# First mixing stage: attention heads one portion later, value products directly behind score products

## The chip, the cores and the metric

The kernel runs on one core of one Trainium2 chip. The metric is the device time of one execution in microseconds (us); smaller is better. A core has TensorE (PE in the profile, with its weight loads as PEld), VectorE (DVE), ScalarE (ACT), GpSimd (POOL) and SyncE (SP), which issues the DMAs. Each engine runs its own instructions in order, and they wait for one another by semaphores.

## The reference, cut to what matters

Two transformer blocks on 256 tokens of width 1024, in float32. The change touches only the mixing stage of the first block, `first_block` in the reference:

```python
h = h + 0.5 * swiglu(rmsnorm(h, ffn1_norm[l]), ffn1_w_gu[l], ffn1_w_down[l])
u = rmsnorm(h, mix_norm[l])
qa, ka, va, qb, kb, vb, qi, ki, wi, g = jnp.split(u @ w_in[l], SPLIT_POINTS, axis=-1)
...
out_a = dsa_attention(qa, ka, va, qi, ki, wi, bias_dsa)   # 8 heads of 64, 64 best keys of each query
out_b = moba_attention(qb, kb, vb, bias_moba)             # 8 heads of 64, plain causal at this length
gates = jax.nn.sigmoid((g + b_gate[l]).astype(jnp.float32)).astype(h.dtype)
g_a, g_b = jnp.split(gates, 2, axis=-1)
mixed = g_a * (out_a @ w_branch_dsa[l]) + g_b * (out_b @ w_branch_moba[l])
h = h + mixed @ w_out[l]
h = h + 0.5 * swiglu(rmsnorm(h, ffn2_norm[l]), ffn2_w_gu[l], ffn2_w_down[l])
```

Each of the 16 heads computes softmax(q k^T / 8 + bias) v with a causal mask. The second block has an attention and a recurrence of its own and is not touched.

## The kernel before, in words

All large products are made of three TensorE products of split operands: ScalarE copies a weight unit to `hi` (line 801), VectorE subtracts to get `lo` (line 1253), and TensorE adds hi*xh, lo*xh and hi*xl (lines 1823 to 1825). A unit is 1 MB, three slots go round, and SP loads a unit when `lo` of the unit three before it is done.

The first mixing stage is the product u @ w_in in 11 chunks of columns, each in 4 **portions**, so 44 portions p = 0 to 43. Portion p is chunk p // 4, half p // 2 % 2 of the contraction, and token tile t = p % 2; on TensorE it is 12 matmuls of 512 columns. Everything else of the stage is hung behind a portion number, and each engine has a loop over the same p with its own steps in an order written out by hand:

- `M1_T`: portions behind which q and k rows are transposed (TensorE line 2049, ScalarE line 993 takes them out). I call such a group M. Two of them stand at 21 and 22, two more at 25 and 26.
- `M1_DOTS`, `M1_TOPK`: the index scores and the 8 rounds of max and replace on VectorE, portions 13 to 20, with a threshold at 21.
- `M1_STEP[k]`: the portion of softmax step k; k = 0 to 7 are the heads of `moba_attention`, 8 to 15 those of `dsa_attention`. Before, it is 20 + k.

For step k the work is spread so (before):

- TensorE, portion 20 + k, k even only: `pair_scores` for heads k and k + 1, 8 matmul passes (lines 1978 to 1982) on halves of 64 rows. I call it S. Its waits ask that the logits of the two steps before are done (`m_l`).
- VectorE, portion 20 + k: `logits`, which adds the bias and takes the row maximum (lines 1403 and 1407), increments `m_l`.
- ScalarE, portion 21 + k: the exponential (line 1042).
- VectorE, portion 22 + k: reciprocal and scaling (lines 1597 and 1599), increments `m_n`.
- TensorE, portion 23 + k: three transposes of the probabilities (line 2080), which wait for `m_n`. I call it T. ScalarE copies them to `pt1` (line 1010), in the same portion.
- TensorE, portion 24 + k, k odd only: `pair_values` for heads k - 1 and k, 8 passes (lines 1993 to 1997) on halves of 64 columns. I call it V. It stands in the code behind T.

`M1_MASK[h]` (22 + h) is the portion in which VectorE adds the key mask to the bias of head h (line 1592). `M1_OUT[j]` (28, 32, 36, 40) is where ScalarE and VectorE take four heads' output out of PSUM (lines 1051 and 1607). VectorE's order within a portion is: logits, head scaling of the projections (`head_scale`, line 1525), head sums (line 1517), gate eviction (1573), max rounds, threshold (1585), mask, reciprocal and scaling, output, and last `lo` of half a unit. ScalarE's is: M out, `pt1`, eviction and square of the projections (1032 and 1036), exponential, output, the sigmoid of portion 39, and last `hi` of half a unit. A chunk's eviction runs in its portions with p % 4 = 2 and 3.

So an even portion from 24 on was followed on TensorE by S and T, and an odd one by T and V. TensorE works in three layouts here: the full array (portions, M, T), two halves of rows (S), two halves of columns (V).

Of the kernel before, what the change touches and what calls it, by code (L numbers as in the profile page):

```python
# [47 lines left out]
NH = 8  # L48
# [50 lines left out]
        (4, 0): 21, (4, 1): 22, (5, 0): 25, (5, 1): 26}  # L99
M1_DOTS = 9  # L100
M1_TOPK = 13
M1_STEP = [20 + k for k in range(2 * NH)]
M1_MASK = [22 + h for h in range(NH)]
M1_OUT = [28, 32, 36, 40]

M2_T = {(c, t): 4 * (c + 1) + 1 + t for c in (0, 1, 3, 4, 5, 7, 8, 9) for t in range(NT)}
M2_STEP = [12, 13, 15, 16, 18, 19, 21, 22, 24, 25, 26, 27, 29, 30, 32, 33]
# [10 lines left out]
def at(seq, p):  # L118

    return seq.index(p) if p in seq else -1  # L120
# [12 lines left out]
def key_at(table, p):  # L133

    for key, when in table.items():
        if when == p:
            return key
    return None
# [65 lines left out]
def program(nc, a, out):  # L204
    ctx = ExitStack()
    with ctx:
        def sem(name):
            return ctx.enter_context(nc.semaphore(name))

        def sb(name, shape, dt=F32, where=ctx):  # L210
            return where.enter_context(nc.sbuf_tensor(name, shape, dt))
# [44 lines left out]
        with scope() as s:  # L256
# [6 lines left out]
            v1 = sb("v1", [P, NT, W], F32, s)  # L263
            v1b = sb("v1b", [P, NT, W], F32, s)
# [114 lines left out]
        m_ev = sem("m_ev")  # L379
# [18 lines left out]
        m_ptc = sem("m_ptc")  # L398
        m_pv = sem("m_pv")
        m_oh = sem("m_oh")  # L400
        m_ol = sem("m_ol")
# [373 lines left out]
        def _(act):  # L775
# [197 lines left out]
            for p in range(4 * len(IN1)):  # L973
# [22 lines left out]
                if M1_DOTS <= p < M1_DOTS + NIDX:  # L996
                    h = p - M1_DOTS
                    act.wait_ge(m_dot, h + 1)
                    if h >= 1:
# [3 lines left out]
                                         scale=HD ** -0.5 * NIDX ** -0.5).then_inc(m_relu, 1)  # L1003
                k = at(M1_STEP, p - 3)
                if k >= 0:
# [5 lines left out]
                if u == 1 and kind != "g":  # L1011
# [15 lines left out]
                    else:  # L1027
# [8 lines left out]
                        nc.scalar.activation(sq, hid[:, t, :], ACT.Square).then_inc(m_sq, 1)  # L1036
                k = at(M1_STEP, p - 1)
                if k >= 0:
# [6 lines left out]
                    e.then_inc(m_p, 1)  # L1045
                j = at(M1_OUT, p)
                if j >= 0:
# [174 lines left out]
        def _(dve):  # L1222
# [304 lines left out]
            for p in range(4 * len(IN1)):  # L1527
# [3 lines left out]
                if M1_DOTS <= p < M1_DOTS + NIDX:  # L1531
# [11 lines left out]
                    dve.wait_ge(m_acc, 2 * h + 2)  # L1543
                k = at(M1_STEP, p)
                if k >= 0:
# [37 lines left out]
                if p == M1_TOPK + TOPK // 8:  # L1583

                    step(nc.vector.tensor_scalar(score[:, :], score[:, :], (FILL + TAKEN) / 2, NEG,
                                                 ALU.is_gt, ALU.mult))
                h = at(M1_MASK, p)
                if h >= 0:
# [3 lines left out]
                    nc.vector.tensor_tensor(bias_a[:, h, :], bias_a[:, h, :], score[:, :], ALU.add).then_inc(m_masked, 1)  # L1592
                k = at(M1_STEP, p - 2)
                if k >= 0:
# [6 lines left out]
                    ins.then_inc(m_n, 1)  # L1601
                j = at(M1_OUT, p)
                if j >= 0:
# [196 lines left out]
        def _(pe):  # L1800
            def use(n, off=0):
                pe.wait_ge(lo_done, n + 1 + RING * off)
# [47 lines left out]
            def turned(r, t, b):  # L1850

                pe.wait_ge(n_xl, 4 * r + ROUNDS[r].index((t, b)) + 1)
# [122 lines left out]
            def pair_scores(qt, qb, kt, kb, done):  # L1975

                upper, lower = slice(0, HD), slice(HD, 2 * HD)
                nc.tensor.matmul(S[0][:, 0:SEQ], qt[upper, qb, P:SEQ], kt[upper, kb, :], start=True, stop=True)  # L1978
                nc.tensor.matmul(S[1][:, 0:SEQ], qt[lower, qb, P:SEQ], kt[lower, kb, :], start=True, stop=True)
                nc.tensor.matmul(S[0][:, SEQ:SPAN], qt[upper, qb, 0:P], kt[upper, kb, 0:P],  # L1980
                                 start=True, stop=True).then_inc(done, 1)
                nc.tensor.matmul(S[1][:, SEQ:SPAN], qt[lower, qb, 0:P], kt[lower, kb, 0:P],
                                 start=True, stop=True).then_inc(done, 1)

            def pair_values(v, k):

                h = k % NH
                o = O[h // 4]
                first = h // 2 % 2 * SEQ
                whole, late = slice(first, first + SEQ), slice(first + P, first + SEQ)  # L1990
                left, right = slice(h * HD, h * HD + HD), slice(h * HD + HD, h * HD + 2 * HD)
                one, two = pt1[:, k % 4, :], pt1[:, k % 4 + 1, :]
                nc.tensor.matmul(o[0:HD, whole], v[:, 0, left], one[:, 0:SEQ], start=True, stop=False)  # L1993
                nc.tensor.matmul(o[HD:P, whole], v[:, 0, right], two[:, 0:SEQ], start=True, stop=False)
                nc.tensor.matmul(o[0:HD, late], v[:, 1, left], one[:, SEQ:SPAN],
                                 start=False, stop=True).then_inc(m_pv, 1)
                nc.tensor.matmul(o[HD:P, late], v[:, 1, right], two[:, SEQ:SPAN],
                                 start=False, stop=True).then_inc(m_pv, 1)
# [13 lines left out]
            for p in range(4 * len(IN1)):  # L2012
                c, u, t = p // 4, p // 2 % 2, p % 2
                if c == 0:

                    u, t = p % 2, p // 2
                    turned(1, t, u)
                _, width, kind = IN1[c]
                n = U_M1 + 2 * c + u
                if t == 0:  # L2020
                    use(n)
                if u == 0 and c > 0:

                    if c <= 7:
                        pe.wait_ge(m_ev, 2 * (c - 1) + t + 1)
                    else:
                        pe.wait_ge(m_gadd, 2 * (c - 8) + t + 1)
                ins = portion(n, t, G[t], xh, xl, 4 * u, u == 0, u == 1, width)
                if t == 1:
                    ins.then_inc(used, 1)  # L2030
                elif u == 1:
                    ins.then_inc(m_g0, 1)
                if c == 0 and t == 0:
                    turn_norm(1, 2 + u)
                key = key_at(M1_T, p)
                if key is not None:
                    cc, tt = key
                    order = list(M1_T).index(key)
                    if order >= 1:
                        pe.wait_ge(m_trev, order)  # L2040
                    if cc == 0:
                        pe.wait_ge(m_ev, tt + 1)
                        for j in range(3):
                            ins = nc.tensor.transpose(X[0][:, j * P:(j + 1) * P], idx[:, tt, j * P:(j + 1) * P],
                                                      ident[:, :])
                    else:
                        pe.wait_ge(m_qn, 2 * (1, 2, 4, 5).index(cc) + tt + 1)
                        for j in range(4):
                            ins = nc.tensor.transpose(X[0][:, j * P:(j + 1) * P], hid[:, tt, j * P:(j + 1) * P],
                                                      ident[:, :])  # L2050
                    ins.then_inc(m_tr, 1)
                if M1_DOTS <= p < M1_DOTS + NIDX and (p - M1_DOTS) % 2 == 0:

                    h = p - M1_DOTS
                    pe.wait_ge(m_trev, 2)
                    if h == 0:
                        pe.wait_ge(res_done, 4)
                    else:
                        pe.wait_ge(m_relu, h)
                    pair_scores(idxt, h // 2, idxt, 2, m_dot)  # L2060
                k = at(M1_STEP, p)
                if k >= 0 and k % 2 == 0:

                    if k == 0:
                        pe.wait_ge(m_relu, NIDX)
                        pe.wait_ge(m_trev, 6)
                    else:
                        pe.wait_ge(m_l, k)
                    if k == NH:
                        pe.wait_ge(m_trev, 10)  # L2070
                    qt, kt = (q_m, k_m) if k < NH else (q_a, k_a)
                    pair_scores(qt, k % NH // 2, kt, k % NH // 2, m_s)
                k = at(M1_STEP, p - 3)
                if k >= 0:

                    pe.wait_ge(m_n, k + 1)
                    if k >= 1:
                        pe.wait_ge(m_ptc, k)
                    for j, b in enumerate((2, 0, 1)):
                        ins = nc.tensor.transpose(PT[:, j * P:(j + 1) * P], l1[:, k % 4, b * P:(b + 1) * P],  # L2080
                                                  ident[:, :])
                    ins.then_inc(m_pt, 1)
                k = at(M1_STEP, p - 4)
                if k >= 0 and k % 2 == 1:

                    pe.wait_ge(m_ptc, k + 1)
                    if k == 1:
                        pe.wait_ge(m_ev, 8)
                    if k == NH + 1:
                        pe.wait_ge(m_ev, 14)  # L2090
                    if k >= NH and k % 4 == 1:
                        pe.wait_ge(m_ol, (k - NH) // 4 + 1)
                    pair_values(v1 if k < NH else v1b, k - 1)


            for q in range(4):
# [40 lines left out]
            for p in range(4 * len(IN2)):  # L2137
# [30 lines left out]
                k = at(M2_STEP, p)  # L2168
                if k >= 0 and k % 2 == 0:
                    h = k // 2  # L2170
# [107 lines left out]
```

## Time and profile before

| | us |
|---|---|
| median of 3 runs | 1003.91 (1003.77 to 1003.92) |
| the profiled execution | 1003.34 |
| its span | 1001.5 |
| PE busy | 992.6 (99%) |
| DVE busy | 688.5 (69%) |
| ACT busy | 548.8 (55%) |

The granted TensorE clock is 1.00 of full speed in the whole execution. The page's 40 slices show PE at 9 tenths in all but the first and the last. The first mixing stage lies between about 205 and 342 us of the span. The timelines give the start and the duration of each instruction; as matmuls overlap, the cost of one is read from the distance of starts and not from its duration.

### The profile page before, as it was taken

What the parts mean: (1) busy time and instruction counts of PE and PEld (TensorE: products, weight loads), DVE (VectorE), ACT (ScalarE), POOL (GpSimd) and SP (SyncE); (2) the same over time, 40 slices, a digit from 0 to 9 for tenths busy, and PEclk for the clock granted to TensorE, in tenths of its full rate; (3) what the DMA queues carried; (4) which work ended last, traced back from release to release, by engine and by line L of the source; (5) the groups of instructions that cost most, each with busy time, mean ns of one, the idle gap of its engine ahead of it and who ended that gap; (6) DMA issues with size and microseconds to landing.
All of it is one profiled execution on the core that took longest, in us unless ns stands there. A gap on an engine that the chain in (4) does not pass through costs nothing.

```text
span 1001.5 us, 12563 instructions
## 1 busy us (share of the span) xinstructions
PE 992.6 (99%) x4626; PEld 814.0 (81%) x4626; DVE 688.5 (69%) x1008; ACT 548.8 (55%) x749; POOL 120.4 (12%) x109
## 2 busy tenths in 40 slices
PE   8999999999999999999999999999999999999998
PEld 7788888888777888888888887888888888888887
DVE  6656666668977567656565667787689767656663
ACT  7444443566766536444444576768875545444541
POOL 0000000022200000000000041258913000000000
PEclk9999999999999999999999999999999999999999
DMA  7987776585434636656666466467556546787761
GB/s 261 296 248 254 236 245 211 194 288 179 143 127 128 208 126 216 226 184 225 198 210 223 134 252 216 129 188 207 150 171 208 195 154 219 224 221 227 224 196 43
DMA packets 158953, 199.87 MB, mean 200 GB/s; under 512 B 49585, under 2 KB 105018, under 8 KB 158778
## 3 DMA queue, kind: packets, MB, share of 16 engines
q1 hardware_dynamic: 158890, 199.24, 62.8%
q8 instruction: 29, 0.48, 0.2%
q14 instruction: 18, 0.15, 0.0%
q10 hardware_dynamic: 16, 0.00, 0.0%
HBM read 182.45 MB, written 5.77 MB: 188 GB/s over the span
## 4 chain that ended last, share of the span: by engine, by line
PE 93%; DVE 3%; DMA 1%; ACT 1%; POOL 1%; issue 0%; SPq 0%; ACTq 0%
PE bank L1823 22%; PE bank L1825 22%; PE bank L1824 22%; PE bank L1928 7%; PE bank L1926 7%; PE bank L1927 7%; PE bank L1836 1%; DMA raw<-in_w_in 1%; PE bank L1978 1%; DVE lo L1253 1%; PE bank L2080 1%; POOL rstd_q L718 1%; PE bank L1993 0%; DMA resid<-in_x 0%; DVE ss_q L1517 0%
## 5 line engine op out<-in xcount | busy, mean ns | idle before, releaser
L1823 PE MATMUL bank<-hi,xh 128*128 128x512 f32 (+1 forms) x944 | 375.4, 398 | 1.4 <-DVE xl L1275 0.8
L1825 PE MATMUL bank<-hi,xl 128*128 128x512 f32 (+1 forms) x944 | 367.1, 389 | 0.0
L1824 PE MATMUL bank<-lo,xh 128*128 128x512 f32 (+1 forms) x944 | 366.6, 388 | 0.0
L1236 DVE TENSOR_TENSOR lo<-raw,hi 128x2048 fp32r<-128x2048 f32 x112 | 256.2, 2289 | 147.9 <-ACT hi L792 147.9
L792 ACT ACTIVATE hi<-raw 128x2048 fp32r<-128x2048 f32 (+1 forms) x116 | 220.5, 1903 | 133.1 <-PE bank L1928 97.0
L1823 PEld LDWEIGHTS bank<-hi,xh 128*128 128x128 f32 x944 | 177.4, 188 | 40.3 <-issue 2.2
L1825 PEld LDWEIGHTS bank<-hi,xl 128*128 128x128 f32 x944 | 177.2, 188 | 37.5
L1824 PEld LDWEIGHTS bank<-lo,xh 128*128 128x128 f32 x944 | 177.6, 188 | 34.5
L1253 DVE TENSOR_TENSOR lo<-raw,hi 128x1024 fp32r<-128x1024 f32 (+1 forms) x108 | 132.4, 1233 | 32.4 <-ACT hi L801 31.6
L1926 PE MATMUL bank<-hi,hh 128*128 128x512 f32 x304 | 118.9, 391 | 0.0
L1928 PE MATMUL bank<-hi,hl 128*128 128x512 f32 x304 | 118.3, 389 | 0.0
L1927 PE MATMUL bank<-lo,hh 128*128 128x512 f32 x304 | 118.3, 389 | 0.0
L801 ACT ACTIVATE hi<-raw 128x1024 fp32r<-128x1024 f32 x100 | 104.0, 1050 | 16.0 <-PE bank L1825 11.7
L866 ACT ACTIVATE hh<-hid_t 128x512 fp32r<-128x512 f32 x34 | 20.7, 629 | 92.6 <-DVE hid_t L1304 92.6
L1928 PEld LDWEIGHTS bank<-hi,hl 128*128 128x128 f32 x304 | 57.1, 188 | 11.9
L1927 PEld LDWEIGHTS bank<-lo,hh 128*128 128x128 f32 x304 | 57.1, 188 | 11.7
L1926 PEld LDWEIGHTS bank<-hi,hh 128*128 128x128 f32 x304 | 57.1, 188 | 11.5
L711 POOL TENSOR_TENSOR small<-small 128x1 f32<-128x1 f32 x10 | 8.4, 848 | 371.7 <-DVE small L1260 353.4
L854 ACT ACTIVATE act_out<-bank,small 128x256 f32<-128x256 f32 x44 | 20.9, 475 | 55.9 <-PE bank L1825 55.2
L718 POOL TENSOR_TENSOR rstd_q<-ss_q,small 128x8 f32<-128x8 f32 x16 | 37.4, 2336 | 90.9 <-DVE ss_q L1519 90.9
L1312 DVE TENSOR_TENSOR hl<-hid_t,hh 128x512 fp32r<-128x512 f32 x34 | 22.9, 691 | 20.8 <-ACT hh L866 20.8
L1287 DVE SCALAR_TENSOR_TENSOR hid<-bank,small,act_out 128x256 f32<-128x256 f32 x44 | 21.1, 480 | 15.1 <-ACT act_out L854 15.1
(262 smaller groups left out, 958.9 us busy)
## 6 DMA issues: line engine op xcount, KB each, us to landing
raw<-in_w_in SPq DMA_DIRECT2D x48, 1024.0 KB
raw<-in_ffn_w_gu SPq DMA_DIRECT2D x84, 512.0 KB
raw<-in_ffn_w_down SPq DMA_DIRECT2D x22, 1024.0 KB
raw<-in_w_up SPq DMA_DIRECT2D x16, 1024.0 KB
raw<-in_w_down SPq DMA_DIRECT2D x16, 1024.0 KB
raw<-in_w_out SPq DMA_DIRECT2D x8, 1024.0 KB
distance_table<-ftab SPq DMA_DIRECT2D x8, 576.0 KB
raw<-in_w_proj_attn SPq DMA_DIRECT2D x4, 1024.0 KB
```

What stands on the lines that cost most here:

```text
L718: nc.gpsimd.tensor_tensor(rstd_q[:, s], ss_q[:, s], minus_half[:, 0:8], ALU.pow).then_inc(rstd_sem, 1)
L792: nc.scalar.activation(hi[s][:, :, 0:width], raw[s][:, :, 0:width], ACT.Copy).then_inc(hi_done, 1)
L801: ins = nc.scalar.activation(hi[s][:, cut, :], raw[s][:, cut, :], ACT.Copy)
L1236: nc.vector.tensor_tensor(lo[s][:, :, 0:width], raw[s][:, :, 0:width], hi[s][:, :, 0:width].bitcast(F32), ALU.subtract).then_inc(lo_done, 1)
L1253: ins = nc.vector.tensor_tensor(lo[s][:, cut, 0:width], raw[s][:, cut, 0:width], hi[s][:, cut, 0:width].bitcast(F32), ALU.subtract)
L1312: nc.vector.tensor_tensor(hl[:, kt, :], hid_t[:, kt, :], hh[:, kt, :].bitcast(F32), ALU.subtract).then_inc(f.hl, 1)
L1823: nc.tensor.matmul(o, sh, wh, start=first and j == 0, stop=False)
L1824: nc.tensor.matmul(o, sh, wl, start=False, stop=False)
L1825: ins = nc.tensor.matmul(o, sl, wh, start=False, stop=last and j == 3)
L1926: nc.tensor.matmul(DB[t][h][:, :], sh, wh, start=begin, stop=False)
L1927: nc.tensor.matmul(DB[t][h][:, :], sh, wl, start=False, stop=False)
L1928: ins = nc.tensor.matmul(DB[t][h][:, :], sl, wh, start=False, stop=end)
```

## The change

Three lists of portion numbers move by one or two, and in TensorE's loop the V block is put in front of the T block and behind portion `M1_STEP[k] + 5` in place of `+ 4`.

```diff
-M1_STEP = [20 + k for k in range(2 * NH)]
-M1_MASK = [22 + h for h in range(NH)]
-M1_OUT = [28, 32, 36, 40]
+M1_STEP = [21 + k for k in range(2 * NH)]
+M1_MASK = [23 + h for h in range(NH)]
+M1_OUT = [30, 34, 38, 42]
...
                     pair_scores(qt, k % NH // 2, kt, k % NH // 2, m_s)
-                k = at(M1_STEP, p - 3)
-                if k >= 0:
-
-                    pe.wait_ge(m_n, k + 1)
-                    if k >= 1:
-                        pe.wait_ge(m_ptc, k)
-                    for j, b in enumerate((2, 0, 1)):
-                        ins = nc.tensor.transpose(PT[:, j * P:(j + 1) * P], l1[:, k % 4, b * P:(b + 1) * P],
-                                                  ident[:, :])
-                    ins.then_inc(m_pt, 1)
-                k = at(M1_STEP, p - 4)
+                k = at(M1_STEP, p - 5)
                 if k >= 0 and k % 2 == 1:
                     pe.wait_ge(m_ptc, k + 1)
...
                     pair_values(v1 if k < NH else v1b, k - 1)
+                k = at(M1_STEP, p - 3)
+                if k >= 0:
+
+                    pe.wait_ge(m_n, k + 1)
+                    if k >= 1:
+                        pe.wait_ge(m_ptc, k)
+                    for j, b in enumerate((2, 0, 1)):
+                        ins = nc.tensor.transpose(PT[:, j * P:(j + 1) * P], l1[:, k % 4, b * P:(b + 1) * P],
+                                                  ident[:, :])
+                    ins.then_inc(m_pt, 1)
```

After it, S stands behind the odd portions 21 to 35, T behind 24 to 39, V behind the odd portions 27 to 41. Behind portions 27, 29, 31, 33 and 35 TensorE has S, V, T in this order, and behind the even ones between them T alone. The instructions and their number are the same.

## Rows read from the trace of the kernel before

**Rows 1.** The page: busy us of each engine, share of the span, instructions.

```profile
PE 992.6 (99%) x4626; PEld 814.0 (81%) x4626; DVE 688.5 (69%) x1008; ACT 548.8 (55%) x749; POOL 120.4 (12%) x109
```

**Rows 2.** Timeline of PE behind portions 28 and 29: start, duration, instruction [idle before].

```profile
283.89 0.50 PE L1823 MATMUL bank<-hi,xh 128*128 128x512 f32 x1
...
286.86 0.48 PE L1978 MATMUL bank<-k_a,q_a 64*128 64x256 f32 x1
...
287.51 0.27 PE L1982 MATMUL bank<-k_a,q_a 64*128 64x128 f32 x1
287.71 0.55 PE L2080 MATMUL bank<-ident,l 128*128 128x128 f32 x3
288.01 0.48 PE L1823 MATMUL bank<-hi,xh 128*128 128x512 f32 x1
...
291.28 0.43 PE L1993 MATMUL bank<-pt,v 128*64 128x256 f32 x1
...
292.08 0.50 PE L1823 MATMUL bank<-hi,xh 128*128 128x512 f32 x1
```

**Rows 3.** Timeline of PE, starts of portions 36 and 37.

```profile
316.58 0.50 PE L1823 MATMUL bank<-hi,xh 128*128 128x512 f32 x1
...
319.68 0.48 PE L1823 MATMUL bank<-hi,xh 128*128 128x512 f32 x1
```

**Rows 4.** Timeline of PE where the heads begin, portions 21 to 24.

```profile
257.32 0.60 PE L2049 MATMUL bank<-ident,hid 128*128 128x128 f32 x4
257.67 0.48 PE L1823 MATMUL bank<-hi,xh 128*128 128x512 f32 x1
...
260.53 0.60 PE L2049 MATMUL bank<-ident,hid 128*128 128x128 f32 x4
261.80 0.48 PE L1978 MATMUL bank<-k_m,q_m 64*128 64x256 f32 x1 [0.67 <-DVE small L1407]
...
265.99 0.55 PE L2080 MATMUL bank<-ident,l 128*128 128x128 f32 x3 [0.32 <-DVE l L1599]
...
270.41 0.55 PE L2080 MATMUL bank<-ident,l 128*128 128x128 f32 x3 [0.28 <-DVE l L1599]
```

**Rows 5.** Timeline of DVE in the same stretch.

```profile
256.98 0.42 DVE L1403 CUSTOM_DVE_ANT_0 l<-bank,bias_m 128x256 f32<-128x256 f32 x1
...
259.76 1.23 DVE L1253 TENSOR_TENSOR lo<-raw,hi 128x1024 fp32r<-128x1024 f32 x1
260.90 0.41 DVE L1403 CUSTOM_DVE_ANT_0 l<-bank,bias_m 128x256 f32<-128x256 f32 x1
...
266.98 0.42 DVE L1403 CUSTOM_DVE_ANT_0 l<-bank,bias_m 128x256 f32<-128x256 f32 x1
...
267.73 0.68 DVE L1525 TENSOR_TENSOR hid<-hid,rstd_q 128x512 f32<-128x512 f32 x1
268.34 0.69 DVE L1517 TENSOR_REDUCE ss_q<-act_out 128x8 f32<-128x512 f32 x1
...
269.14 0.55 DVE L1592 TENSOR_TENSOR bias_a<-bias_a,score 128x384 f32<-128x384 f32 x1
269.61 0.16 DVE L1597 RECIPROCAL small<-small 128x2 f32<-128x2 f32 x1
```

**Rows 6.** Timeline of ACT in the same stretch.

```profile
257.95 0.69 ACT L993 ACTIVATE q_a<-bank,cols 128x512 f32<-128x512 f32 x1 [3.73 <-PE bank L2049]
258.66 1.28 ACT L1042 ACT_TABLE_LOAD   x1
259.95 0.51 ACT L1042 ACTIVATE l<-l,small 128x256 f32<-128x256 f32 x1
...
260.85 1.04 ACT L801 ACTIVATE hi<-raw 128x1024 fp32r<-128x1024 f32 x1
...
262.36 0.67 ACT L1032 ACTIVATE hid<-bank,small 128x512 f32<-128x512 f32 x1
263.07 0.63 ACT L1036 ACTIVATE act_out<-hid 128x512 f32<-128x512 f32 x1
```

**Rows 7.** Timeline of DVE: its first wait once the heads run.

```profile
279.64 0.42 DVE L1403 CUSTOM_DVE_ANT_0 l<-bank,bias_m 128x256 f32<-128x256 f32 x1 [1.30 <-PE bank L1982]
```

More of the change, by code:

```diff
@@ L2072, in _ @@
                     pair_scores(qt, k % NH // 2, kt, k % NH // 2, m_s)
+                k = at(M1_STEP, p - 5)
+                if k >= 0 and k % 2 == 1:
+                    pe.wait_ge(m_ptc, k + 1)
+                    if k == 1:
+                        pe.wait_ge(m_ev, 8)
+                    if k == NH + 1:
+                        pe.wait_ge(m_ev, 14)
+                    if k >= NH and k % 4 == 1:
+                        pe.wait_ge(m_ol, (k - NH) // 4 + 1)
+                    pair_values(v1 if k < NH else v1b, k - 1)
                 k = at(M1_STEP, p - 3)
@@ L2082, in _ @@
                     ins.then_inc(m_pt, 1)
-                k = at(M1_STEP, p - 4)
[L2084 to L2093, printed above, removed]
             for q in range(4):
```

## The prediction

> **What bounds the kernel now.** I read the page first: TensorE is busy 99% of the span and no other engine passes 69% [rows 1]. So a microsecond of TensorE time, work or stall, is one of the kernel, unless something else then ends last. The change adds and removes no instruction, which leaves two things to look for: what TensorE pays for passing from one array layout to another, and where it stands idle. The timeline of PE answers both.
>
> In the steady part [rows 2] the last score pass starts at 287.51 and the transposes 0.20 later, at 287.71, though that pass has only 128 columns, against the 512 that a portion's matmul moves in 0.23: S pays an exit. Going in costs too: from the first matmul of portion 28 (283.89) to the first score pass (286.86) are 2.97, where 12 matmuls of about 0.23 would take 2.73, and 0.13 to 0.16 of the rest is the slower first matmul behind V. T and the entry into V are still dearer: the values start at 291.28, 3.27 behind the portion's first matmul at 288.01, and the next portion starts 0.80 behind them (292.08).
>
> Where the heads begin, TensorE waits three times [rows 4]: S of step 2 (261.80) waits 0.67 for the logits, T of step 0 (265.99) and T of step 1 (270.41) wait 0.32 and 0.28 for the scaled probabilities. Counted from the start of their portions with the distances above, the two T are late by 0.47 and 0.35, so the three waits cost 1.5 in all. They end at VectorE, whose timeline has no gap in this stretch [rows 5]; its first wait comes at 279.64 [rows 7]. So in the steady part TensorE sets the pace, and in the fill, 255 to 275 us, VectorE does. The two halves of the change must be costed there separately.
>
> **Part 1: V next to S, steady part.** Before, a pair of portions costs 292.08 - 283.89 = 8.19 [rows 2]: S, T, then T, V. After, an odd portion has S, V, T and an even one T alone. T alone is a row: 319.68 - 316.58 = 3.10 [rows 3]. The odd one is put together: portion up to S 2.95 (2.97 less a little, since a portion now follows T and not V), S from first to last pass 0.65, then x for the step from row halves to column halves, V 0.60 from first to last pass and 0.20 out (0.80 together), T to the next portion 0.30 (288.01 - 287.71). That is 4.70 + x, and the pair 7.80 + x. The gain is 0.39 - x.
>
> No row shows x. Its low end is 0, V starting on top of the last score pass; its high end is 0.40, two exits of 0.20 in a row. The nearest row is the exit from S into T, also a change of layout from the same passes, 0.20 [rows 2]. I take 0.21. The gain is then about 0.17 for a pair, and S and V meet behind five portions: 0.85. Behind 37 and 39, V then T takes what T then V took, since each has one entry and one exit of V: no gain, no loss. With the ends of x, Part 1 is worth between 0 and 1.9.
>
> On this the Trainium skill, "TensorEngine Tiling (Array Packing)", section Key Properties, says that a change of tiling mode drains TensorE. The 0.20 exits agree. By that rule S to V, from 64 by 128 to 128 by 64, is again a drain, so one change of four is saved and not two: it speaks for x near 0.20 and against its low end.
>
> **Part 2: everything one portion later, the fill.** One could hope that VectorE, which is behind because of the max rounds (portions 13 to 20), catches up when the heads come one portion later, and that the 1.5 of waits goes. I follow the instructions.
>
> TensorE: portion 21 starts without S of step 0 in front of it. M of portion 21, then S, and portion 22 starts at 257.6, where it also started before (257.67) [rows 4], as S has only changed places with M. M of portion 22 is at 260.5, portion 23 starts 0.35 behind it (257.67 - 257.32) at 260.84. S of step 2 comes at 263.8, and VectorE has the logits of step 1 by then: it starts portion 20's work at 256.98, now without the 0.75 of logits, so `lo` of portion 20 starts at 259.0 (259.76 less 0.75) and ends at 260.15; logits of step 0 (0.75), the threshold, `lo` (1.14) and logits of step 1 (0.75) follow, done by about 263.2 [rows 5]. The wait of 0.67 is gone. Portion 24 starts at 264.6, and T of step 0 could be issued at 267.5.
>
> ScalarE: the exponential of step 0 moves from portion 21 to portion 22. In portion 21 there was nothing between M's copy and it; portion 22 also holds an eviction and a square. And the first exponential brings the table load of 1.28 with it [rows 6]. So, in portion 22: M's copy 0.63 behind M (257.95 - 257.32), 261.1; eviction 261.7; square 0.71 later (263.07 - 262.36), 262.4; table load 262.9; exponential 1.29 later, 264.2; `hi` 0.90 later (260.85 - 259.95), 265.1; it ends at 266.2. ScalarE was idle before that, from its `hi` of portion 21, done at about 258.4, to 261.1, but its queue is in order and the load stands behind M's copy.
>
> VectorE: it has done head sums of portion 22 at 264.0, and its next instruction is `lo` of portion 22, which needs that `hi`. It starts at 266.2, not at 264.0: 2.2 idle, and the lead is spent. `lo` takes 1.14 (260.90 - 259.76): 267.3. Then, for portion 23, by the distances of rows 5: logits of step 2 0.75 (268.1), head scaling 0.61 (268.7), head sums 0.80 (269.5), mask 0.47 (270.0), reciprocal and scaling to the transposes 0.80 (270.41 in rows 4 less 269.61): T of step 0 starts at 270.8. TensorE could have at 267.5, so it waits 3.3.
>
> Before, the portion of VectorE that T of step 0 waited for had no head scaling in it. So this T comes about when T of step 1 came before (270.41 [rows 4]).
>
> After that I find no stall: S of step 4 at 274.5 needs logits of step 3 (272.5); T of step 1 at 275.3 could start from 274.4; T of step 2 at 278.9 has its input at about 277.3; from then on VectorE is 1 to 2 ahead at every T. In the odd portions ScalarE now stays longer behind T (V is in front of it), so `hi` and `lo` come some 1 later, but they are due four portions ahead. At the end, sigmoid and T meet in ScalarE's portion 39: `lo` for the first unit behind the stage is done near 337.5, 5 before its use. The fill costs 3.3 - 1.5 = 1.8 more.
>
> **Sum.** +1.8 - 0.85 = +0.95; a count of portion starts up to portion 43, with 4.91 and 3.10 in turn, gives +0.85. I take +0.9. Against the profiled execution (1003.34, span 1001.5 and 1.84 around it) this is 1004.2. The median of the runs is 0.57 above the profiled execution, and I forecast the median: 1003.9 + 0.9 = 1004.8.
>
> **The rivals.**
>
> *VectorE catches up.* If the table load is issued while ScalarE is idle before 261.1, or something else lets `hi` of portion 22 come by 264, T of step 0 is ready at 268.6, and the fill wait is 1.1 in place of 3.3. Then the fill gains 0.4, and with Part 1 the time is 1003.9 - 1.25 = 1002.7. If no wait at all is left, 1003.9 - 1.5 - 0.85 = 1001.6. For it: the heads do get 3 us more. Against: both the load and the copy stand in one in-order queue. Chance 0.17 for 1002.7 and 0.07 for 1001.6.
>
> *S next to V buys nothing or costs.* x = 0.40 makes the time 1003.9 + 1.8 = 1005.7. Chance 0.10.
>
> *The wait costs more than itself.* This is the one that ends measurably slower. The longest wait shown on TensorE in the fill is 0.67 [rows 4], with the clock at full level; one of 3.3 is new, and nothing here shows that the granted clock of 2.4 GHz survives it. If the portion behind it ran at 1.2 GHz, 2.9 of work would take 2.9 more: 1007.7. It decides as soon as the wait is long enough for the clock to fall. Chance 0.06. The Trainium skill, "TensorE: Matmul & The Clock Gate", section on HAM oscillation, says that idle gaps between bursts throttle the engine again; no run here shows it. A second chain of the same kind (head sums of portion 23 late as well, so T of step 1 late too) gives 1 to 2 more, 1006.3: chance 0.08.
>
> The forecast itself has 0.52.
>
> **How the numbers follow.** About 0.2%, 2.0 us here, is what a measurement of this kernel can tell from no change. Faster than 1001.9: the last form of the first rival and a little of its neighbour, 0.09. Slower than 1005.9: the clock, the second chain and the edge of x = 0.40, 0.15. The rest, 0.76, is within. The range leaves out the no-wait case below and the clock case above: 1002.1 to 1006.4.
>
> **What would show it.** Right: in PE's timeline one wait of about 3 us at the transposes behind portion 24, released by VectorE's scaling, and no wait at S of step 2; in ACT's, the table load behind the square near 262.9; in DVE's, an idle of about 2 before `lo` of portion 22, released by `hi`; portion pairs from 27 on 8.0 apart, and 0.2 from the last score pass to the first value pass. Wrong: no wait above 1.5 in the fill, a table load before 261, pairs of 8.2 or 7.8, a granted clock below 1.00 near 270, or new waits at portions 28 to 43.

## The result and the profile after

| | us |
|---|---|
| before, median of 15 runs | 1003.60 (1002.98 to 1004.20) |
| after, median of 15 runs | 1005.96 (1004.36 to 1008.00) |
| ratio | 1.0024, 95% interval 1.0017 to 1.0031 |
| after, the profiled execution | 1007.63 (span 1005.8, mean granted clock 0.996) |

The kernel became slower by 2.4 us. The median hides a spread: these 15 runs of before lie within 1.2 us, those of after within 3.6. Every run also lists its mean granted TensorE clock. Five of the 15 executions after have 1.000 and take 1004.36 to 1004.84, median 1004.48. The other ten have 0.996 to 0.998 and take 1005.05 to 1008.00. So there are two costs: 0.9 us that each execution pays, and up to 3.5 more that only some pay.

The page of the profiled execution, which is one of the slower kind: the busy line that answers to [rows 1], and, in 40 slices of 25 us, the busy tenths of PE and the granted clock.

```profile
PE 995.2 (99%) x4626; PEld 816.8 (81%) x4626; DVE 689.3 (69%) x1008; ACT 548.6 (55%) x749; POOL 120.1 (12%) x109
...
PE   8999999999899999999999999999999999999998
...
PEclk9999999999899999999999999999999999999999
```

Before, the clock row was all 9. After, it has an 8 in the eleventh slice, 251 to 277 us, and there PE's busy share falls as well. The list of TensorE's waits (us in total, times, longest) shows what is there. The two waits of before at L2080 and the one at L1978 [rows 4] are gone, and one of 3.2 has come (L2091 is the transposes' new line):

```profile
PE bank L2091 <- DVE l L1599: 3.2, 1, 3.2
PE bank L1965 <- POOL small L706: 1.8, 1, 1.8
PE bank L1836 <- DMA resid<-in_x: 1.0, 1, 1.0
```

This execution reaches the stage later than the profiled one before, for nothing that the change touches: the first transposes of the stage (L2044) start at 211.39, before at 210.62. So 0.77 has to be taken off its times before they are laid beside those of before or of the forecast.

The timeline of PE at the start of the heads, against [rows 4]: portion 22 begins at 258.37, S of step 2 at 264.51 has no wait, T of step 0 has the long one, and behind it the matmuls start 0.43 apart in place of 0.23.

```profile
256.99 0.60 PE L2049 MATMUL bank<-ident,hid 128*128 128x128 f32 x4
257.51 0.48 PE L1978 MATMUL bank<-k_m,q_m 64*128 64x256 f32 x1
...
258.37 0.50 PE L1823 MATMUL bank<-hi,xh 128*128 128x512 f32 x1
...
261.23 0.60 PE L2049 MATMUL bank<-ident,hid 128*128 128x128 f32 x4
...
264.51 0.48 PE L1978 MATMUL bank<-k_m,q_m 64*128 64x256 f32 x1
...
271.62 0.90 PE L2091 MATMUL bank<-ident,l 128*128 128x128 f32 x3 [3.23 <-DVE l L1599]
272.18 0.78 PE L1823 MATMUL bank<-hi,xh 128*128 128x512 f32 x1
...
274.03 0.63 PE L1824 MATMUL bank<-lo,xh 128*128 128x512 f32 x1
274.46 0.63 PE L1825 MATMUL bank<-hi,xl 128*128 128x512 f32 x1
...
278.05 0.48 PE L1978 MATMUL bank<-k_m,q_m 64*128 64x256 f32 x1
```

ScalarE's timeline, against [rows 6]: the table load now stands behind the square of portion 22, and `hi` of that portion starts only at 266.00.

```profile
261.86 0.69 ACT L993 ACTIVATE q_a<-bank,cols 128x512 f32<-128x512 f32 x1 [2.60 <-PE bank L2049]
262.45 0.68 ACT L1032 ACTIVATE hid<-bank,small 128x512 f32<-128x512 f32 x1
263.16 0.63 ACT L1036 ACTIVATE act_out<-hid 128x512 f32<-128x512 f32 x1
263.81 1.28 ACT L1042 ACT_TABLE_LOAD   x1
...
266.00 1.04 ACT L801 ACTIVATE hi<-raw 128x1024 fp32r<-128x1024 f32 x1
```

VectorE's timeline, against [rows 5]: it waits 2.23 for that `hi`, and then does head scaling, head sums and mask before the reciprocal at 270.83.

```profile
264.67 0.17 DVE L1519 TENSOR_SCALAR ss_q<-ss_q 128x8 f32<-128x8 f32 x1
267.07 1.23 DVE L1253 TENSOR_TENSOR lo<-raw,hi 128x1024 fp32r<-128x1024 f32 x1 [2.23 <-ACT hi L801]
...
268.96 0.69 DVE L1525 TENSOR_TENSOR hid<-hid,rstd_q 128x512 f32<-128x512 f32 x1
...
270.83 0.16 DVE L1597 RECIPROCAL small<-small 128x2 f32<-128x2 f32 x1
```

The steady part, against [rows 2] and [rows 3]: two portions take 298.69 - 290.69 = 8.00 in place of 8.19, the first value pass starts 0.20 behind the last score pass, and T 0.20 behind the last value pass.

```profile
290.69 0.47 PE L1823 MATMUL bank<-hi,xh 128*128 128x512 f32 x1
...
294.28 0.27 PE L1982 MATMUL bank<-k_a,q_a 64*128 64x128 f32 x1
294.48 0.43 PE L1993 MATMUL bank<-pt,v 128*64 128x256 f32 x1
...
295.08 0.27 PE L1997 MATMUL bank<-pt,v 128*64 128x128 f32 x1
295.28 0.55 PE L2091 MATMUL bank<-ident,l 128*128 128x128 f32 x3
...
298.69 0.47 PE L1823 MATMUL bank<-hi,xh 128*128 128x512 f32 x1
```

Last the clock. The busy times of two stretches of 4 us in the changed kernel; the clock is the number 0.60 and 0.55 ahead of the DMA share. Before, all stretches read 1.00.

```profile
270.00:274.00 4.00, 2.38 (x7) 2.02 (x8) 3.90 (x14) 1.54 (x7) 1.87 (x1) 0.60 0.64 241
274.00:278.00 4.00, 4.00 (x13) 2.97 (x11) 2.28 (x6) 0.87 (x1) 0.00 (x0) 0.55 0.16 19
```

A mean of 0.60 over 4 us is 3.2 us at half the clock, a mean of 0.55 is 3.6. So TensorE went to its lower level of 1.2 GHz at about 270.8, towards the end of the wait, after it had been idle since 268.4. It stayed there for the rest of the wait and the whole portion behind it, 6.8 us in all, and was back at 2.4 GHz by S of step 4.

### The profile page after: what moved, and what is told of

The parts are those of the page before. It is cut to its first block, busy times and chain, and to the rows that moved or that the text cites. A ratio compares the mean times of both kernels' runs of the same rounds, so it can differ in the third digit from the quotient of the medians.

```text
span 1005.8 us, 12563 instructions
## 1 busy us (share of the span) xinstructions
PE 995.2 (99%) x4626; PEld 816.8 (81%) x4626; DVE 689.3 (69%) x1008; ACT 548.6 (55%) x749; POOL 120.1 (12%) x109
## 4 chain that ended last, share of the span: by engine, by line
PE 96%; DVE 1%; ACT 1%; POOL 0%; DMA 0%; issue 0%; SPq 0%; ACTq 0%
PE bank L1823 23%; PE bank L1825 23%; PE bank L1824 23%; PE bank L1928 7%; PE bank L1927 7%; PE bank L1926 7%; PE bank L1836 1%; PE bank L1978 1%; PE bank L2091 1%; PE bank L1993 0%; DMA resid<-in_x 0%; PE bank L2049 0%; PE bank L1980 0%; DVE lo L1253 0%; PE bank L2212 0%; PE bank L2213 0%
```

## The experiments

The first four were measured together with the kernel before (its median: 1003.51 of 31 runs, from 1002.76 to 1005.04), the last three in a second series (1003.64 of 25, from 1002.99 to 1004.56). The kernel before spreads over 2.3 us in the first of these at clocks of 0.999 and 1.000, so a wide spread alone is no sign of a fallen clock; the clock listed with each run is. Each ratio is against the kernel before of the same series.

**The shift alone.** The order of T and V as before, the heads one portion later.

```diff
-M1_STEP = [20 + k for k in range(2 * NH)]
-M1_MASK = [22 + h for h in range(NH)]
-M1_OUT = [28, 32, 36, 40]
+M1_STEP = [21 + k for k in range(2 * NH)]
+M1_MASK = [23 + h for h in range(NH)]
+M1_OUT = [29, 33, 37, 41]
```

> Heads one portion later, but the value products behind the transposes as before (portion M1_STEP + 4, outputs at 29, 33, 37, 41). Theory (fill costs 1.8 more, adjacency gains 0.85): T of step 0 waits about 3.2 us, S of step 2 does not wait, portion pairs stay 8.2 apart; 1005.4 us where the clock stays at full level, 2 to 3 more where it falls, median about 1007. Rival (the shift itself is harmless, the new order of S, V and T costs): 1003.6 us and no clock below 1.00.

Measured: median 1006.48 (1005.16 to 1006.86, 9 runs), ratio 1.0025 [1.0015, 1.0035]. Four runs with clock 1.000 take 1005.16 to 1006.00, five with 0.998 take 1006.48 to 1006.86. The wait is in place, in an execution whose clock stayed at 1.00; there T of step 0 at 271.71 is followed by S of step 4 at 275.39, 3.68 later, where the changed kernel's slowed execution needed 278.05 - 271.62 = 6.43 for the same work.

```profile
271.71 0.55 PE L2080 MATMUL bank<-ident,l 128*128 128x128 f32 x3 [3.23 <-DVE l L1599]
...
275.39 0.48 PE L1978 MATMUL bank<-k_m,q_m 64*128 64x256 f32 x1
```

The whole loss is in the shift, and the clock falls without S and V being neighbours, so the rival, that the new order costs, is out. What was expected of the slower executions did not come: their median lies 1.2 above that of the four with clock 1.000, not 2 to 3, and so the median is 1006.48 and not about 1007. In the changed kernel the same distance is 2.4. Why a fallen clock costs less here is not shown, and the samples are small.

**The new order alone.**

```diff
-M1_STEP = [21 + k for k in range(2 * NH)]
-M1_MASK = [23 + h for h in range(NH)]
-M1_OUT = [30, 34, 38, 42]
+M1_STEP = [20 + k for k in range(2 * NH)]
+M1_MASK = [22 + h for h in range(NH)]
+M1_OUT = [29, 33, 37, 41]
```

(against the changed kernel)

> Heads where they were before (M1_STEP = 20 + k, masks 22 + h), only the value products moved to M1_STEP + 5 in front of the transposes (outputs at 29, 33, 37, 41). Theory: the three short waits of before stay (0.67, 0.32, 0.28 by the profile), five pairs cost 8.0 in place of 8.17 to 8.2, the clock stays at 1.00: 1003.6 - 0.85 = 1002.8 us. Rival (adjacency is what costs or what lets the clock fall): 1003.6 to 1006 us with clocks below 1.00.

Measured: 1002.87 (1002.21 to 1003.45), ratio 0.9993 [0.9984, 1.0002], clocks 0.999 and 1.000. The medians are 0.64 apart, near the 0.85 expected, but the interval holds 1, so by the times alone the gain is not shown. The trace does show its parts: the three waits of before and nothing else, and the portions behind two successive groups of S, V and T start 8.00 apart, at 287.47 and 295.47.

```profile
261.66 0.48 PE L1978 MATMUL bank<-k_m,q_m 64*128 64x256 f32 x1 [0.68 <-DVE small L1407]
265.85 0.55 PE L2091 MATMUL bank<-ident,l 128*128 128x128 f32 x3 [0.31 <-DVE l L1599]
270.27 0.55 PE L2091 MATMUL bank<-ident,l 128*128 128x128 f32 x3 [0.24 <-DVE l L1599]
...
287.47 0.48 PE L1823 MATMUL bank<-hi,xh 128*128 128x512 f32 x1
...
295.47 0.47 PE L1823 MATMUL bank<-hi,xh 128*128 128x512 f32 x1
```

**The wait filled with work.** This and the next three are edits of the changed kernel. Twelve matmuls whose results nothing reads, ahead of the wait of T of step 0.

```diff
                 if k >= 0:

+                    if k == 0:
+                        for d in range(12):
+                            nc.tensor.matmul(O[1][:, :], xh[:, d % 4, 0:P], hi[(U_M1 + 12) % RING][:, d % 4, :],
+                                             start=True, stop=True)
                     pe.wait_ge(m_n, k + 1)
```

> The changed kernel, with 12 more full matmuls (128 rows, 128 by 512, results into a bank that nothing reads) issued by TensorE in front of the wait of T of step 0, so that it computes 2.7 of the 3.3 us in which it would be idle. Theory (the clock falls because TensorE is idle for 3.2 us): granted clock 1.000 in every execution, about 1004.5 us, spread like that of the kernel before (about 1 us). Rival (the clock falls for something else in the new order, or the spread has nothing to do with it): clocks of 0.996 to 0.998 in most executions again, median 1006.

Measured: 1004.29 (1003.85 to 1005.50), ratio 1.0009 [1.0000, 1.0018], clock 1.000 in all 11 runs. The runs lie within 1.7 us, about 1 was expected, and those of before in the same series within 2.3. T of step 0 comes 271.43 - 256.80 = 14.63 behind M of portion 21, exactly as in the changed kernel (271.62 - 256.99), so nothing was saved but the idling:

```profile
268.04 2.88 PE L2089 MATMUL bank<-hi,xh 128*128 128x512 f32 x12
271.43 0.55 PE L2095 MATMUL bank<-ident,l 128*128 128x128 f32 x3 [0.51 <-DVE l L1599]
```

More work on TensorE made the kernel 1.6 us faster (0.8 over the kernel before, in place of 2.4). The lower clock of the changed kernel comes from TensorE standing idle for 3.2 us. What is left is near the forecast of +0.9, but its interval reaches from 0 to 1.8 us.

**The table load moved to where ScalarE is idle.**

```diff
                 mixing_split(split_hi_part, U_M1, p)
+                if p == 21:
+                    nc.scalar.activation(small[:, 23:24], ident[:, 0:1], ACT.Exp)
```

> The changed kernel, with one exponential of a single column more on ScalarE at the end of portion 21, where it is idle, so that the table load of 1.28 us does not stand in portion 22 in front of the first half unit of hi. Theory (hi of portion 22 is late by the table load and by the exponential): VectorE's idle before lo of portion 22 falls from 2.2 to 0.9, T of step 0 waits 1.9 to 2.0 in place of 3.2; 1003.2 us, and the clock stays at 1.00 in all or nearly all executions. Rival (VectorE's own work sets T of step 0): the wait stays above 3 us, 1004.5 to 1006.

Measured: 1002.88 (1002.36 to 1004.37), ratio 0.9993 [0.9984, 1.0002], clocks 0.999 and 1.000. The median is 0.3 under the 1003.2 expected. The load stands at 258.60, VectorE's idle ahead of `lo` of portion 22 is 0.81 (2.23 in the changed kernel), and T of step 0 waits 1.81, a little less than the 1.9 to 2.0 expected:

```profile
258.60 1.28 ACT L1060 ACT_TABLE_LOAD   x1
...
261.19 0.69 ACT L993 ACTIVATE q_a<-bank,cols 128x512 f32<-128x512 f32 x1 [1.09 <-PE bank L2051]
...
263.91 1.04 ACT L801 ACTIVATE hi<-raw 128x1024 fp32r<-128x1024 f32 x1
```

```profile
264.98 1.23 DVE L1255 TENSOR_TENSOR lo<-raw,hi 128x1024 fp32r<-128x1024 f32 x1 [0.81 <-ACT hi L801]
```

`hi` starts 263.91 - 261.19 = 2.72 behind the copy of M of portion 22, in the changed kernel 266.00 - 261.86 = 4.14, so it comes 1.42 earlier. Both idle times fell by 1.42 too: what ScalarE's queue is rid of, VectorE no longer idles and TensorE no longer waits. One instruction on one column is worth 3 us in the median. Of this 1.4 is the wait; the rest is what the clock had cost, the 1.6 that filling the wait gave back as well.

**The scaling right behind the logits.** VectorE's loop, the block for `at(M1_STEP, p - 2)` moved up.

```diff
                     logits(S[k % 2], l1[:, k % 4, :], bias, k, m_l)
+                k = at(M1_STEP, p - 2)
+                if k >= 0:
+                    dve.wait_ge(m_p, k + 1)
+                    step(nc.vector.reciprocal(inv[:, 2 * k:2 * k + 2], sums[:, 2 * k:2 * k + 2]))
+                    ...
+                    ins.then_inc(m_n, 1)
                 if p >= 1 and (p - 1) // 4 in (1, 2, 4, 5) and (p - 1) // 2 % 2 == 1:
                     head_scale(2 * (1, 2, 4, 5).index((p - 1) // 4) + (p - 1) % 2, (p - 1) % 2, m_qn, m_rstd)
```

> The changed kernel, with VectorE's reciprocal and scaling moved from behind head scaling, head sums and mask to right behind the logits of the portion. Theory (T of step 0 waits for a queue in order: those three stand in front of what it needs, 0.61 + 0.80 + 0.47 = 1.9): the wait falls from 3.2 to 1.4, the time to 1002.6 us, and the clock stays at 1.00 as in the kernel with the early table load, whose wait was 1.8. Rival (the scaling itself waits for the exponential, or the displaced work makes a later wait): wait above 2.5, or new waits behind portions 25 to 30; 1003.5 or more.

Measured: 1002.99 (1001.97 to 1003.83), ratio 0.9992 [0.9983, 1.0001], clocks 0.999 and 1.000. The wait is 1.37 as expected, and no other one came; the median is 0.4 over what was expected, within the spread of the runs.

```profile
269.47 0.55 PE L2091 MATMUL bank<-ident,l 128*128 128x128 f32 x3 [1.37 <-DVE l L1564]
```

**Both together**, the two diffs above in one kernel.

> The changed kernel with both: the early table load and the scaling right behind the logits. Theory: the two take 1.4 and 1.9 from the wait of 3.2, so that none is left; no wait of TensorE at all in portions 21 to 43; 1001.1 us, 2.4 below the kernel before (of which 1.5 are its three waits and 0.85 the five pairs). Rival (another input is late next, the max rounds or a head scaling): 1002 us or more, with a named wait in the trace.

Measured: 1001.22 (1000.95 to 1002.28, 9 runs), ratio 0.9977 [0.9967, 0.9987], clock 1.000 in all. T of step 0 starts at 267.85 without a wait, and the whole list of TensorE's waits has only those of other stages:

```profile
PE bank L1967 <- POOL small L706: 1.8, 1, 1.8
PE bank L1838 <- DMA resid<-in_x: 1.2, 1, 1.2
PE bank L1825 <- DVE xl L1277: 0.8, 2, 0.6
PE bank L1825 <- DVE lo L1255: 0.6, 2, 0.4
```

This is the fastest version, within 0.1 of the 1001.1 expected: 2.4 us under the kernel before, 4.7 under the changed one.

**The new order and the early scaling, heads where they were**: the diff of the new order alone, and that of the early scaling.

> Heads where they were before, value products in front of the transposes (as in the adjacent-only kernel), and the scaling right behind the logits. Theory: the waits of T of steps 0 and 1 (0.47 and 0.35 by distances) go, the wait of S of step 2 (0.68) stays, since nothing in front of those logits has moved: 1002.9 - 0.8 = 1002.1 us. Rival (VectorE is simply out of time here, so the lag shows up one step later): 1002.9 us.

Measured: 1001.83 (1001.22 to 1003.51), ratio 0.9981 [0.9972, 0.9990]. The waits of both T are gone, that of S of step 2 stays, as expected; the median is 0.3 under the 1002.1 expected:

```profile
261.95 0.48 PE L1978 MATMUL bank<-k_m,q_m 64*128 64x256 f32 x1 [0.67 <-DVE small L1407]
```

So three quarters of the best version's gain need no shift at all.

## Why the prediction was right, and where it was off

**Part 1** held. The step from S to V was taken at 0.21 and is 0.20 (294.48 - 294.28); a pair was put at 8.01 and is 8.00. The shift alone and the changed kernel, which differ in this part alone, stand at a median of 1005.39 (four runs) and 1004.48 (five runs) where the clock is 1.000: 0.9, against 0.85. The runs come from two series, each near 1003.5 for the kernel before. These are a few runs each, and the new order alone is 0.64 under the kernel before with an interval that holds no change, so the times agree with 0.85 and do not show it by themselves; the distances in the traces do. One change of layout in four is saved. S to V and V to T take 0.20 each, where two passes of 128 columns within S start 0.11 apart. The Trainium skill, "TensorEngine Tiling (Array Packing)", Key Properties, says that a change of tiling mode drains TensorE; the trace agrees for the change from S straight to V.

**Part 2** held, link by link. With 0.77 taken off, portion 22 starts at 257.60 (forecast 257.6), `lo` of portion 22 at 266.30 (266.2) and T of step 0 at 270.85 (270.8). No wait for S of step 2. The table load at 2.6 behind M of portion 22 (forecast 2.4). VectorE idle for 2.23 (2.2). T of step 0 waits 3.23 (3.3), and nothing waits after it, up to portion 43. The early table load and the early scaling take the two links out one by one, by 1.42 and 1.86, and together leave none.

**The sum** held where TensorE keeps its clock: +0.88 measured (1004.48 against 1003.60), +0.9 forecast.

**The first rival** came true in the early table load, but was priced too well. It took the wait to 1.1 and the time to 1.25 under the kernel before. The wait is 1.81 and the time 0.6 under: moving the load frees only 1.42 of ScalarE's queue, and `hi`, which still has the exponential in front of it, ends after the head sums all the same (VectorE idle for 0.81).

**What was off is the clock.** The forecast priced the long wait at its own length, and gave the case in which it costs more a chance of 0.06. It happened in 10 of 15 executions, and in 5 of 9 of the shift alone. The median therefore lies 1.2 above the forecast of 1004.8, or 1.5 by the difference, as 15 runs put the kernel before 0.3 under the three that the forecast started from. It is 2.4 above the kernel before, just past the 0.2% from which a change can be told: slower, which had a chance of 0.15, where no measurable change had 0.76. That the median still lies in the range of 1002.1 to 1006.4 is luck: the range was drawn to leave this case out, seven of the 15 executions lie above it, and the median is inside because a third kept the clock and some of the others lost little. The mechanism of that rival was right, and its price for the profiled execution: 2.9 more for the portion behind the wait was forecast, and it lost 6.43 - 3.68 = 2.75 between T of step 0 and S of step 4. Over all ten slowed executions the median loss is 2.4. That the profiled time, 1007.63, nearly meets the 1007.7 of this rival is chance, since 0.77 of it was lost ahead of the stage. What was mis-sized is the chance of this term, and with it the nothing that the sum has for it. The prediction itself gave the reason for more: the longest wait within the fill that the rows showed was 0.67, so nothing in them spoke for a clock that survives 3.3. The Trainium skill, "TensorE: Matmul & The Clock Gate", section on HAM oscillation, warns of idle gaps between bursts; the rows agree, and here the gap lets the clock fall in most executions and not in all.

What stays open is why the loss spreads from 0.5 to 3.5 in the slowed executions. The mean clocks point to the length of the stretch at the lower level: the five with 0.998 take 1005.05 to 1006.92, the five with 0.997 or 0.996 take 1006.91 to 1008.00. Only one of them was profiled, so it is not shown whether in the milder ones the clock fell later or rose sooner. Nor is it shown why some executions kept the clock through the same wait.

## What to carry to other kernels

When a stage is moved against portions of another, the fill is where the move is decided: follow each in-order queue through the first two steps, one-time items such as a table load included, since an item that was hidden in an idle stretch can land ahead of something that three engines wait for. On a TensorE that is otherwise always busy, a wait of a few microseconds has two prices, its length and the clock behind it; shorten it, or fill it with matmuls whose results nothing reads, and look at the clock of every run and not only at the median time. And a change of layout saved is worth 0.2 us here, so five of them do not pay for a wait of 3.2.

## What the runs showed of the hardware

- The same wait of 3.23 us on TensorE went by at full clock in one profiled execution (the shift alone) and came with 6.8 us at 1.2 GHz in another (the changed kernel). By the mean clocks, 10 of 15 and 5 of 9 executions of these two kernels lost clock. With longest waits in this stage of 1.81, 1.37 and 0.68 us no execution lies below 0.999, in 11 each, and the kernel before lists 0.999 at times as well.
- TensorE passing directly from two tiles of 64 rows to two tiles of 64 columns takes the same 0.20 us, from the start of the last pass to the start of the next instruction, as passing from either to the full array.
- The table load costs the queue 1.28 us and little more: with it out of the way, `hi` came 1.42 earlier, counted from the copy ahead of it. The Trainium skill, "ScalarE: Activation LUTs", section What ACT_TABLE_LOAD costs, gives 1283 ns for the load and 1380 ns of drain with it; the trace agrees with the first and shows no more than 0.14 of the second.
